# Four feed-forward entrances: token terms through PSUM, plain hidden products inside the units

## The reference

```
for l in range(2):
    x = x + 0.5 * swiglu(rmsnorm(x, ffn1_norm[l]), ffn1_w_gate[l], ffn1_w_up[l], ffn1_w_down[l])
    h = rmsnorm(x, mix_norm[l])
    x = x + concat(ssd_mixer(h @ w_in[l]), hgrn2_mixer(h @ w_in[l])) @ w_out[l]
    x = x + 0.5 * swiglu(rmsnorm(x, ffn2_norm[l]), ffn2_w_gate[l], ffn2_w_up[l], ffn2_w_down[l])
out = rmsnorm(x, final_norm)
# swiglu(h, g, u, d) = (silu(h @ g) * (h @ u)) @ d ; g, u: 1024 x 2816, d: 2816 x 1024
```

## Time and profile before

| | us |
|---|---|
| median of 3 runs | 1980.73 |
| lowest and highest | 1979.98, 1984.19 |
| the profiled execution, its own time | 1980.09 |
| its span in the trace | 1978.2 |
| PE busy in it | 1883.8 |
| DVE, ACT, POOL busy | 1190.0, 946.1, 1065.4 |

### The profile page before, as it was taken

How to read it: one execution, slowest core, us unless ns; L and a number is a source line. 1 busy time by engine, 2 the same in 40 slices (tenths; PEclk the granted TensorE clock), 3 DMA queues, 4 the chain that set the end, 5 groups by cost and what they waited for, 6 DMA issues and landing times.

```text
span 1978.2 us, 36545 instructions
## 1 busy us (share of the span) xinstructions
PE 1883.8 (95%) x12988; PEld 1670.2 (84%) x12988; DVE 1190.0 (60%) x1924; ACT 946.1 (48%) x1599; POOL 1065.4 (54%) x806
## 2 busy tenths in 40 slices
PE   7699999999999699999988999999999996999999
PEld 6698899787788599899867989987877885988997
DVE  7762475478777863266377615745868777623653
ACT  5463365474544364265435524645546434633654
POOL 2565465565335565466436645655634445654654
PEclk9899999999999899999998999999999998999999
DMA  4133233422122133333322332333222121332333
GB/s 151 65 102 104 94 108 95 130 65 77 65 65 85 51 102 116 90 107 97 114 66 75 106 111 88 103 100 114 77 75 65 65 86 64 99 108 94 108 95 119
DMA packets 58200, 182.93 MB, mean 92 GB/s; under 512 B 7328, under 2 KB 7328, under 8 KB 58016
## 3 DMA queue, kind: packets, MB, share of 16 engines
q1 hardware_dynamic: 57872, 180.56, 28.9%
q10 hardware_dynamic: 144, 0.00, 0.0%
HBM read 178.45 MB, written 2.10 MB: 91 GB/s over the span
## 4 chain that ended last, share of the span: by engine, by line
PE 88%; DVE 6%; issue 4%; ACT 2%; DMA 0%; DVEq 0%; ACTq 0%
PE ps L1938 15%; PE ps L1939 15%; PE ps L1940 15%; PE ps L2045 12%; PE ps L2047 12%; PE ps L2049 12%; DVE u L1305 1%; DVE terms L1276 1%; DVE terms L1278 1%; PE ps L2220 1%; PE ps L2137 1%; PE ps L2139 1%; PE ps L2138 1%; ACT thi L721 1%; PE ps L2268 0%
## 5 line engine op out<-in xcount | busy, mean ns | idle before, releaser
L2045 PE MATMUL ps<-thi,whi 128*128 128x256 f32 x2016 | 574.1, 285 | 38.2 <-DVE u L1300 38.2
L2047 PE MATMUL ps<-tlo,whi 128*128 128x256 f32 x2016 | 573.4, 284 | 0.0
L2049 PE MATMUL ps<-thi,wlo 128*128 128x256 f32 x2016 | 573.4, 284 | 0.0
L586 POOL TENSOR_TENSOR wlo<-raw,whi 128x768 fp32r<-128x768 f32 (+2 forms) x168 | 323.3, 1933 | 355.6 <-ACT whi L713 318.0
L2045 PEld LDWEIGHTS ps<-thi,whi 128*128 128x128 f32 x2016 | 390.4, 194 | 40.2 <-issue 39.7
L599 POOL TENSOR_TENSOR wlo<-raw,whi 128x512 fp32r<-128x512 f32 x216 | 278.5, 1302 | 257.2 <-ACT whi L765 257.2
L2047 PEld LDWEIGHTS ps<-tlo,whi 128*128 128x128 f32 x2016 | 390.3, 194 | 0.5
L2049 PEld LDWEIGHTS ps<-thi,wlo 128*128 128x128 f32 x2016 | 390.0, 193 | 0.0
L579 POOL TENSOR_TENSOR wlo<-raw,whi 128x256 fp32r<-128x256 f32 x256 | 222.3, 900 | 221.7 <-ACT whi L713 221.7
L713 ACT ACTIVATE whi<-raw 128x1024 fp32r<-128x1024 f32 (+2 forms) x200 | 184.9, 926 | 260.5 <-PE ps L1940 241.2
L1938 PE MATMUL ps<-hhi,whi 128*128 128x512 f32 x608 | 248.5, 409 | 41.4 <-POOL wlo L586 39.3
(11 more groups left out here) (323 smaller groups left out, 3177.4 us busy)
## 6 DMA issues: line engine op xcount, KB each, us to landing
raw<-in_up SPq DMA_DIRECT2D x168, 512.0 KB, 3.5
raw<-in_mix SPq DMA_DIRECT2D x64, 512.0 KB, 3.5
raw<-in_dn SPq DMA_DIRECT2D x64, 384.0 KB, 3.1
raw<-in_dn SPq DMA_DIRECT2D x64, 320.0 KB, 2.9
raw<-in_lead SPq DMA_DIRECT2D x8, 512.0 KB, 3.6
x<-in_x SPq DMA_DIRECT2D x8, 256.0 KB, 5.7
raw<-in_lead SPq DMA_DIRECT2D x8, 256.0 KB, 5.9
raw<-in_mix SPq DMA_DIRECT2D x8, 256.0 KB, 2.6
```

The costliest lines, as they stand in the source:

```text
L586: pool.tensor_tensor(wlo[:, q, 0:width], raw[:, q, 0:width], whi[:, q, 0:width].bitcast(F32), ALU.subtract).then_inc(split.sem, 1)
L2045: mm(bank(dst)[:, 0:HT], wh[:, s], thi[c][:, k, cols], start=start and k == 0, stop=False, skip_group_check=True)
L2047: mm(bank(dst)[:, 0:HT], wh[:, s], tlo[c][:, k, cols], start=False, stop=False, skip_group_check=True)
L2049: last = mm(bank(dst)[:, 0:HT], wl[:, s], thi[c][:, k, cols], start=False, stop=k == KH - 1, skip_group_check=True)
```

## The change

In every entrance:

- Of the terms of one k, B11, T3, B21 and B22 are now made in PSUM, in banks 5 and 7 (`TERM_BANKS`), and B12, T1, T2, T4 in SBUF (four buffers, one per k). The norm is read from its PSUM bank instead of `r`. As there is one pair of banks, `make_terms(k)` waits for DVE's low part of k - 1.
- ACT makes the high parts of the PSUM pieces (1024 columns, event `mixed_high`) and of the SBUF pieces (768 columns, `terms_high`) in two instructions. DVE makes the low part of the former and POOL that of the latter, for all four k.
- The plain gate and up results get buffers of their own (`plain_g`, `plain_u`, `plain_h`). `plain_hidden`, its high and its low part (`plain_hidden_hi`, `plain_hidden_lo`) leave the entrance and are issued in units 4 to 8.
- POOL's and ACT's orders are rewritten: ACT makes the high parts of blocks 4 to 6 before the first silu.
- Turns and spreads of the norm are placed by the count of tile products: behind 6 and 13 (first part of a layer), 8 and 15 (second part), 25 and 30 (the very first).

```diff
-T1, T3, T2, T4, B21, B22, B11, B12 = range(8)
+T1, T2, T4, B11, T3, B21, B22 = range(7)
+B12 = 3
+TERM_BANKS = (5, 7)
...
-        terms = [[lay(f"terms{c}_{i}", [P, 8, HT], (HERE[c] + 48, 112)[i]) for i in range(2)] for c in range(2)]
+        TEMP = [(HERE[c] + 48, HERE[c] + 52, 112, 116) for c in range(2)]
+        terms = [[lay(f"terms{c}_{k}", [P, 4, HT], TEMP[c][k]) for k in range(KH)] for c in range(2)]
...
                 def terms_low(k):
                     pool.wait_ge(terms_high.sem, terms_high.upto(l, KH * c + k))
-                    pool.tensor_tensor(tlo[c][:, k, :], terms[c][k % 2][:, 0:TERMS, :].rearrange("p i t -> p (i t)"),
-                                       thi[c][:, k, :].bitcast(F32), ALU.subtract).then_inc(terms_low_pool.sem, 1)
+                    pool.tensor_tensor(tlo[c][:, k, 0:B11 * HT],
+                                       terms[c][k][:, 0:B11, :].rearrange("p i t -> p (i t)"),
+                                       thi[c][:, k, 0:B11 * HT].bitcast(F32), ALU.subtract)\
+                        .then_inc(terms_low_pool.sem, 1)
...
                 def prepare(u):
                     low_a11(u)
                     make_s3(u)
+                    if u == PLAIN:
+                        terms_low(3)
                     low_a12(u)
                     low_s3(u)
 
-                for b in range(NS, 2 * PLAIN):
-                    low(l, wb + b)
-                    if b >= 2 * PLAIN - 2:
-                        terms_low(b - 2 * PLAIN + KH)
+                low(l, wb + 4)
+                low(l, wb + 5)
+                terms_low(0)
+                low(l, wb + 6)
+                low(l, wb + 7)
+                terms_low(1)
+                terms_low(2)
...
                     def terms_hi(k):
                         act.wait_ge(terms_made.sem, terms_made.upto(l, KH * c + k))
-                        act.activation(thi[c][:, k, :], terms[c][k % 2][:, 0:TERMS, :].rearrange("p i t -> p (i t)"),
+                        act.activation(thi[c][:, k, B11 * HT:].rearrange("p (b t) -> p b t", t=T), term_banks(),
+                                       ACT.Copy).then_inc(mixed_high.sem, 1)
+                        act.activation(thi[c][:, k, 0:B11 * HT],
+                                       terms[c][k][:, 0:B11, :].rearrange("p i t -> p (i t)"),
                                        ACT.Copy).then_inc(terms_high.sem, 1)
...
                     terms_hi(0)
                     hi(wb + 4)
+                    hi(wb + 5)
+                    hi(wb + 6)
                     plain_silu(0)
-                    hi(wb + 5)
                     terms_hi(1)
+                    hi(wb + 7)
+                    terms_hi(2)
                     plain_silu(1)
-                    hi(wb + 6)
-                    hi(wb + 7)
-                    hidden_hi(0)
-                    terms_hi(2)
-                    hidden_hi(1)
+                    slot_hi(PLAIN, A11)
                     terms_hi(3)
...
                             if u > u0:
                                 hidden_hi(u - 1)
+                                if u <= 2 * PLAIN:
+                                    plain_hidden_hi(u - 1 - PLAIN)
...
                     def make_terms(k):
-                        t = terms[c][k % 2]
-                        if k >= 2:
-                            ready(terms_low_dve, 2 * c + k - 2)
-                        did(stt(t[:, B21:B22 + 1, :].rearrange("p i t -> p (i t)"), x[:, KH + k, :], gain(KH + k), r[:],
-                                ALU.mult, ALU.mult))
-                        did(stt(t[:, B11:B12 + 1, :].rearrange("p i t -> p (i t)"), x[:, k, :], gain(k), r[:],
-                                ALU.mult, ALU.mult))
+                        t, first_bank, second_bank = terms[c][k], bank(TERM_BANKS[0]), bank(TERM_BANKS[1])
+                        b11, t3 = first_bank[:, 0:HT], first_bank[:, HT:T]
+                        b21, b22 = second_bank[:, 0:HT], second_bank[:, HT:T]
+                        if k:
+                            ready(terms_low_dve, KH * c + k - 1)
+                        did(stt(second_bank, x[:, KH + k, :], gain(KH + k), bank(NORM), ALU.mult, ALU.mult))
+                        did(stt(b11, x[:, k, 0:HT], gain(k), bank(NORM)[:, 0:HT], ALU.mult, ALU.mult))
+                        did(stt(t[:, B12, :], x[:, k, HT:T], gain(k), bank(NORM)[:, HT:T], ALU.mult, ALU.mult))
                         settle()
-                        did(tt(t[:, T1, :], t[:, B12, :], t[:, B11, :], ALU.subtract))
-                        did(tt(t[:, T3, :], t[:, B22, :], t[:, B12, :], ALU.subtract))
+                        did(tt(t[:, T1, :], t[:, B12, :], b11, ALU.subtract))
+                        did(tt(t3, b22, t[:, B12, :], ALU.subtract))
                         settle()
-                        did(tt(t[:, T2, :], t[:, B22, :], t[:, T1, :], ALU.subtract))
+                        did(tt(t[:, T2, :], b22, t[:, T1, :], ALU.subtract))
                         settle()
-                        made(terms_made, tt(t[:, T4, :], t[:, B21, :], t[:, T2, :], ALU.subtract))
+                        made(terms_made, tt(t[:, T4, :], b21, t[:, T2, :], ALU.subtract))
 
                     def terms_low(k):
-                        ready(terms_high, KH * c + k)
-                        made(terms_low_dve, tt(tlo[c][:, k, :],
-                                               terms[c][k % 2][:, 0:TERMS, :].rearrange("p i t -> p (i t)"),
-                                               thi[c][:, k, :].bitcast(F32), ALU.subtract))
+                        ready(mixed_high, KH * c + k)
+                        made(terms_low_dve, tt(tlo[c][:, k, B11 * HT:].rearrange("p (b t) -> p b t", t=T), term_banks(),
+                                               thi[c][:, k, B11 * HT:].bitcast(F32).rearrange("p (b t) -> p b t", t=T),
+                                               ALU.subtract))
...
                         elif n == 1:
                             loaded_block(b)
                             ready(sum_made, 3 * v)
+                            if u == PLAIN:
+                                ready(terms_low_dve, KH * c + KH - 1)
...
                     make_terms(0)
                     plain_gate(0)
                     terms_low(0)
+                    make_terms(1)
                     plain_up(0)
-                    make_terms(1)
+                    terms_low(1)
+                    make_terms(2)
                     plain_gate(1)
                     plain_up(1)
-                    terms_low(1)
-                    plain_hidden(0)
-                    hidden_lo(0)
-                    make_terms(2)
-                    plain_hidden(1)
-                    hidden_lo(1)
+                    terms_low(2)
                     make_terms(3)
                     plain_gate(2)
                     make_sum(PLAIN, 0)
+                    terms_low(3)
                     plain_up(2)
-                    plain_hidden(2)
-                    hidden_lo(2)
...
                                 hidden_lo(u - 1)
+                                if u <= 2 * PLAIN:
+                                    plain_hidden_lo(u - 1 - PLAIN)
...
                             hidden_second(u)
+                            if u < 2 * PLAIN:
+                                plain_hidden(u - PLAIN)
...
-                    turns_at, spreads_at = (KD - 2, KD) if (l, c) == (0, 0) else (3, 5)
+                    turns_at, spreads_at = (25, 30) if (l, c) == (0, 0) else (8, 15) if c else (6, 13)
```

More of the change, by code:

```diff
@@ L223, in trunk_kernel @@
         early_lo = [lay(f"early_lo{c}", [P, PLAIN, T], HERE[c] + 40, F32R) for c in range(2)]
[L224 removed]
+        TEMP = [(HERE[c] + 48, HERE[c] + 52, 112, 116) for c in range(2)]
+        terms = [[lay(f"terms{c}_{k}", [P, 4, HT], TEMP[c][k]) for k in range(KH)] for c in range(2)]
+        plain_g = [lay(f"plain_g{c}", [P, PLAIN, T], HERE[c] + 40) for c in range(2)]
+        plain_u = [lay(f"plain_u{c}", [P, PLAIN, T], HERE[c] + 32) for c in range(2)]
+        plain_h = [[lay(f"plain_h{c}_{j}", [P, T], TEMP[c][j]) for j in range(PLAIN)] for c in range(2)]
         thi = [lay(f"thi{c}", [P, KH, TERMS * HT], THERE[c], F32R) for c in range(2)]
@@ L1307, in hidden_lo, with plain_hidden_lo @@
-                    def hidden_lo(j):
-                        ready(hid_high, NJ * c + j)
-                        made(hid_low, tt(hid_lo_tile(c, j), u2[:, j % 2, :], hid_hi_tile(c, j).bitcast(F32),
+                        ready(plain_silu_g, PLAIN * c + j)
+                        ready(terms_low_pool, KH * c + j)
+                        made(plain_hid, tt(plain_h[c][j][:], plain_g[c][:, j, :], plain_u[c][:, j, :], ALU.mult))
+                    def plain_hidden_lo(j):
+                        ready(plain_high, PLAIN * c + j)
+                        made(plain_low, tt(hid_lo_tile(c, j), plain_h[c][j][:], hid_hi_tile(c, j).bitcast(F32),
+                                           ALU.subtract))
```

(24 more changed lines are left out.)

55 lines of the change are left out of this document (30 added, 25 removed).

## The result

| | before | after |
|---|---|---|
| median | 1981.07 us (4 runs) | 1903.52 us (4 runs) |
| lowest and highest | 1979.98, 1984.19 | 1902.61, 1908.46 |
| the profiled execution, its span | 1980.09, 1978.2 | 1902.61, 1900.9 |

What follows compares the result with a forecast made beforehand. PE, busy 95%, was held by entrance waits for GpSimd low parts and VectorE's last plain_up: 95.5 us with clock loss. 17.1 stays, 78.4 won from 1980.1 gives 1901.7, about 1902 us median; range 1893 to 1930, own 1895 to 1911.

Steps and rivals of the forecast that it cites:

- What can be won: Entrances of the four feed-forward parts: 77.5 us of PE waits plus 18 us of lowered clock, 95.5 us in all.
- The mechanism of the holds: In the entrances, VectorE instructions with two SBUF inputs and running GpSimd ones exclude each other; holds of 2 to 3 us.
- The early norm: Norm moved forward in the entrances: no PE wait in second and fourth parts, a new 1.1 us in the third.
- The terms: Making terms in the entrances: 3.05 us per make_terms, low parts 1.22 us on VectorE, 1.86 on GpSimd.
- VectorE's slack before unit 4: Entrance's end: VectorE takes 28.6 us from the norm copy, has 4 to spare; PE waits 1.0 us, not 9.4 to 9.9.
- Into the units: Plain_hidden work moved to units 4 to 8: PE waits 0.13 us per unit for VectorE's up_second, 0.5 per entrance.
- The rival in which VectorE bounds the units by 20 us: Units 5 to 8: VectorE becomes the bound, both holds in all 16 units add 20 us, 1922 us; chance 0.25.
- The other rivals: Forward norm makes PE wait at the spreads, 1908 us, 0.07; slower serial terms, 0.04; unchanged, 0.02.
- The serial terms: Entrances: make_terms waits for the preceding low part; step at most 5.4 us, costs above 7.5; slower, chance 0.04.
- the slower case: Terms steps in the entrances above about 12.5 us make the kernel slower; 1988 us at 13 us; chance 0.04.
- the one without gain: Waits in the entrances only move, PE finding block 4 or 7 as late as before: 1980 us, chance 0.02.
- Clock: Entrances: granted clock 1.00 in second and fourth parts; 2.0 us lost behind the first part's first wait; 1.0 us waits harmless.

Runs made afterwards that it cites:

- e3_norm_sbuf: Changed kernel with the three make_terms multiplications reading the norm from its SBUF copy instead of PSUM: 1941.55 us, ratio 0.9795.
- e2_old_norm: Changed kernel with the norm's turns and spreads back at their old positions: 1903.66 us, ratio 0.9602 against the kernel before.
- The later runs: For the 1.78 and 2.19 waits: changed kernel with block 4's high part before the first terms' high part on ScalarE, 1901.11 us.
- the second run: Repeat of the changed kernel with old norm positions, ScalarE's block high parts earlier and plain_hidden behind the second sum: 1896.12 us.

## Why the prediction was right, step by step

- **What can be won (95.5 us), of which 17.1 stays.** Measured in the profile after: waits 7.93 + 0.88 + 0.87 + 0.87 + 0.88 + 0.73 = 12.2, clock about 2 behind A's first wait, units 4 x 0.65 = 2.6; 16.8 together. 95.5 - 16.8 = 78.7; the two spans differ by 77.3, and the start of the kernel alone moves by about 1 us between executions.
- **The mechanism of the holds** was argued from a few rows; `e3_norm_sbuf` shows it, by one operand, at 38 us. That the plain part's cost would be for the most part ScalarE and the list itself once the terms are new, the prediction did not say.
- **The early norm.** That it gives PE no wait in B and about 1 us in C (0.73) was right. For B it left 0.55 and 1.7 us of slack beside the 0.65 of transposes: 1.20 and 2.34, which the rows of reduce (1.20) and copy (2.35) have to within 0.01. That it is worth nothing was not foreseen as such: the sum gave it no term of gain and charged 1.1 us for C. `e2_old_norm` shows that with the new terms this is all there is.
- **The terms.** A 256-column write into PSUM is not 0.41: the three-operand form takes 0.48, the plain one 0.42, and at 512 columns 0.75 and not 0.68 (the kernel before already had 0.75 for this form, unheld, at 635.40). `make_terms(0)` takes 3.24 us (615.65 to 618.89), not 3.05. The low part at 1.22 and GpSimd's at 1.85 were right (predicted 1.22, 1.86).
- **VectorE's slack before unit 4** was the worst sized step: of "4 us to spare" 0.70 were idle in front of the last `plain_up` of B. It took 32.7 us from copy to ready, not 28.6. The difference is not work but waiting for ScalarE and PE: 1.50 for block 0, 3.02 before the second low part (ScalarE waits 1.48 and 0.98 for PE's blocks and loads a table for 1.28), 0.67 and 0.74 for slots. VectorE is paced by PE's blocks through ScalarE and not by the copy, which is why `e2_old_norm` can have the copy 2 us later for nothing: the waits on the way take it up, so that the real room is at least 2 us more than the 0.70. The step's result, about 1 us of wait (0.87), stood all the same, since the last `plain_up` waited for PE.
- **Into the units.** 0.5 us per part predicted, 0.65 measured, so the size was nearly right; the place was not. The prediction had PE wait for VectorE's `up_second`; the rows have it stop for ScalarE's copy, behind the plain high part, a term that the step put at nothing. The rival in which VectorE bounds the units by 20 us did not come: one VectorE instruction per unit is held for long (1.79 at 658.89, 670.06, 680.37, 690.67), not two.
- **The other rivals.** No wait of PE at the spreads of B or D. The serial terms never were the last to end, but their steps are longer than the "at most 5.4 us": 6.6, 8.1, 5.6 and 5.6 in B, the first two with the idle 1.50 and 3.02 in them. The second passes the 7.5 from which the prediction let a step cost, and costs nothing, since that bound holds for all four together (25.9 us, with some of the plain gates and ups in them). By the same terms 13 us per step would give 1990 us and not the 1988 that stands there, which changes nothing. Neither the slower case nor the one without gain has a row.
- **Clock.** 1.00 through B and D as predicted; A's first wait costs its 2 us. That a wait of 1.0 is too short to lower the clock did not follow from the earlier trace rows, which have only 0.54 and 7.80; it came true (1.00 behind 0.87 and 0.88). The later runs have 1.00 behind 1.78 and a lowered clock behind 2.19.

## What to carry to other kernels

Where a VectorE row is two or more times as long as the same shape elsewhere, look at which GpSimd instruction ended just before the row's own end. Moving one of the row's two SBUF inputs to PSUM can be worth as much as a large reordering (38 us here for one operand, 48 for putting off the plain part), even at one more instruction; work that cannot be moved so goes to where nobody waits for it. A step moved ahead of its consumer gives nothing if the chain is paced by another engine: read who ends its idle time before moving it.

## What was not expected of the hardware

- The hold strikes 256-column instructions of 0.4 us as fully as long ones: 0.42 became 4.08, next to one GpSimd instruction of 4.13. The Trainium skill (GPSIMD Engine Reference, Key points) has the shared interface and the contention; by this rule, the trace agrees. How long a hold is, only the rows tell: up to the whole GpSimd instruction.
- A product of three operands on VectorE costs 0.06 us more than one of two, at 256 as at 512 columns (0.48 and 0.42, 0.75 and 0.69).
- A wait of 2.2 to 2.6 us costs nearly as much clock as one of 8: 1.7 us, against 1.9. In these runs the clock is still full when PE resumes and falls only later (1.2 us behind the 2.19, 1.5 and, in the second run, 0.3 behind the 2.60), so that the first matmuls behind the wait can look sound. Behind waits of 0.9 to 1.8 us it stayed 1.00 in each stretch looked at.
